# A gated convolution and memory-attention layer: another order for the requests, squares and streamed rows of its output projection, and for its first requests

## What is computed

```
h    = rms_norm(x, pre_norm)
proj = h @ w_in                                 # 1024 -> 3*1024 + 1536 + 512
b, c, u = split(proj[:, :3072]);  z = c * u
mix  = b * (w0*z[t-2] + w1*z[t-1] + w2*z[t])    # short causal convolution
mem_o = softmax(mq @ k.T / sqrt(128)) @ v       # 4 heads over 256 memory rows
y    = (concat(mix, mem_o) * silu(gate)) @ w_out    # 1536 -> 1024
out  = x + rms_norm(y, post_norm)
```

## Time and profile before

| | |
|---|---|
| timed, median of 3 | 2169.3 us (2167.65 to 2175.27) |
| profiled execution | 2171.62 us, span 2169.8 us |
| TensorE matmuls | busy 2150.4 us, 99% of the span, 9792 |
| TensorE weight loads | busy 1781.7 us, 82%, beside the matmuls |
| VectorE | busy 1216.5 us, 56% |
| ScalarE | busy 753.5 us, 35% |
| GpSimd | busy 222.3 us, 10% |
| moved by DMA | 550.35 MB, mean 254 GB/s |

### The profile page before, as it was taken

How to read it: one execution, slowest core, us unless ns; L and a number is a source line. 1 busy time by engine, 2 the same in 40 slices (tenths; PEclk the granted TensorE clock), 3 DMA queues, 4 the chain that set the end, 5 groups by cost and what they waited for, 6 DMA issues and landing times. The chain is left out here.

```text
span 2169.8 us, 26681 instructions
## 1 busy us (share of the span) xinstructions
PE 2150.4 (99%) x9792; PEld 1781.7 (82%) x9792; DVE 1216.5 (56%) x1840; ACT 753.5 (35%) x1330; POOL 222.3 (10%) x377
## 2 busy tenths in 40 slices
PE   9999999999999999999999999999999999999998
PEld 7888888888888888888888888888888788888787
DVE  7858777533335353354345337575754756555565
ACT  6544333411221342221123234535442533333333
POOL 0100000000000111111111000101010111111110
PEclk9999999999999999999999999999999999999999
DMA  7798777677776778998877666666568866665665
GB/s 272 273 328 299 284 269 275 239 247 243 267 231 219 278 255 292 324 328 284 289 239 258 242 222 202 217 196 222 192 207 317 321 223 237 251 244 210 232 230 191
DMA packets 165057, 550.35 MB, mean 254 GB/s; under 512 B 20224, under 2 KB 20256, under 8 KB 164032
## 3 DMA queue, kind: packets, MB, share of 16 engines
q1 hardware_dynamic: 128528, 416.34, 55.3%
q0 software_dynamic: 36400, 132.31, 17.3%
HBM read 404.90 MB, written 143.67 MB: 253 GB/s over the span
## 5 line engine op out<-in xcount | busy, mean ns | idle before, releaser
L1900 PE MATMUL banks<-hop_hi,slots 128*128 128x512 f32 x2184 | 852.0, 390 | 0.5 <-DMA slots<-w_split 0.4
L1901 PE MATMUL banks<-hop_lo,slots 128*128 128x512 f32 x2184 | 850.2, 389 | 0.0
L1902 PE MATMUL banks<-hop_hi,slots 128*128 128x512 f32 x2184 | 849.9, 389 | 0.0
L1900 PEld LDWEIGHTS banks<-hop_hi,slots 128*128 128x128 f32 x2184 | 410.2, 188 | 86.1 <-issue 0.9
L1902 PEld LDWEIGHTS banks<-hop_hi,slots 128*128 128x128 f32 x2184 | 410.0, 188 | 85.5
L1901 PEld LDWEIGHTS banks<-hop_lo,slots 128*128 128x128 f32 x2184 | 410.2, 188 | 82.9
L1900 PE MATMUL banks<-hop_hi,out_slot 128*128 128x512 f32 x448 | 176.1, 393 | 5.1 <-ACT mix L1075 2.0
L1902 PE MATMUL banks<-hop_hi,out_slot 128*128 128x512 f32 x448 | 175.9, 393 | 0.0
L1901 PE MATMUL banks<-hop_lo,out_slot 128*128 128x512 f32 x448 | 175.7, 392 | 0.0
L1489 DVE TENSOR_TENSOR out_slot<-out_raws,out_slot 128x768 fp32r<-128x768 f32 x112 | 107.2, 957 | 100.4 <-ACT out_slot L1000 100.4
L1546 DVE TENSOR_TENSOR u<-banks,u 128x512 f32<-128x512 f32 x54 | 37.3, 690 | 205.8 <-PE banks L1902 205.7
(11 more groups left out here) (206 smaller groups left out, 2720.0 us busy)
## 6 DMA issues: line engine op xcount, KB each, us to landing
slots<-w_split SPq DMA_DIRECT2D x406, 512.0 KB, 4.3
w_split<-slots SPq DMA_DIRECT2D x140, 512.0 KB, 3.5
mw_stream<-mw_kept SPq DMA_DIRECT2D x96, 512.0 KB, 4.6
out_raws<-g_kept POOLq DMA_DIRECT2D x60, 384.0 KB, 6.1
raws<-in_w_in SPq DMA_DIRECT2D x82, 256.0 KB, 5.0
g_kept<-mix POOLq DMA_DIRECT2D x64, 256.0 KB, 5.1
x_res<-in_x POOLq DMA_DIRECT2D x32, 512.0 KB, 5.6
out_x<-x_res POOLq DMA_DIRECT2D x31, 512.0 KB, 3.5
```

The lines of the kernel that those rows point to most:

```text
L1900: nc.tensor.matmul(dst, a, c, start=first, stop=False, skip_group_check=True)
L1901: nc.tensor.matmul(dst, a, d, start=False, stop=False, skip_group_check=True)
L1902: return nc.tensor.matmul(dst, b, c, start=False, stop=last, skip_group_check=True)
```

## The change

The order of requests, of squares and of streamed rows is changed; no arithmetic is.

- TensorE's small matmuls go from 26 to 14, and wait only for `ones`, which VectorE sets in its first instruction. The gains and the weight blocks X11 of pairs 0 and 1 are requested by ScalarE ahead of its other work; the taps by GpSimd after its constants, and they are waited for only where the first convolution needs them. The first piece of x is split ahead of the first weight block.
- The four squares of token tile 0 all come after both halves of the R6 operand; on VectorE the weight sums of R3 and R7 go behind the low halves of R6, and the last weight block's low part between two pairs of norms.
- `mw_stream` has three places, used round by round for single tiles; in each streamed unit one tile is used first and the other ahead of the last tile. SyncE requests tile 0 of (pair 0, R3) and the operand of R4 right after the last unit of the input projection.
- ScalarE and VectorE split the R4 operand in step 4, ahead of the weight block built in that step.
- On GpSimd the four blocks of pair j+1 come ahead of both residual requests, with the store of tile 2j-1 after the first.
- The post norm's gains lie at the place of `junk` and are requested near the end of the last macro; `junk` is in PSUM.

```diff
-WARM = 26
+WARM = 14
-STREAMED = {R5: 0, R3: 2, R2: 3}
-STREAM = [(j, r) for j in range(OUT_PAIRS) for r in STREAMED]
+STREAMED = (R5, R3, R2)
+STREAM = [(j, r, k) for j in range(OUT_PAIRS) for r in STREAMED for k in range(HB)]
...
-        mw_stream = at("mw_stream", Z_AT, [HB, 2, HALF], f32r)
+        mw_stream = [at(f"mw_stream{n}", offset, [2, HALF], f32r) for n, offset in enumerate((Z_AT, Z_AT + 4 * KB, 118 * KB))]
-        junk = at("junk", S_AT, [2, HALF])
+        junk = psum[:, 4:6, :]
...
+            def load_stream(j, r, k):
+                n = STREAM.index((j, r, k))
+                place = n % len(mw_stream)
+                if n >= len(mw_stream):
+                    sp.wait_ge(mw_used, n - len(mw_stream) + 1)
+                sp.dma_start(mw_stream[place][:].bitcast(f32), mw_kept[r, k]).then_inc(mw_stream_dma[place], 16)
...
-            load_first_x(0, 0)
-            load_raw(0, X11)
-            for n in (1, 2, 3):
+            for n in range(HK):
                 load_first_x(0, n)
-            load_raw(1, X11)
...
             for r in (R6, R3, R7, R2):
                 load_out(r)
+            sp.wait_ge(unit_done, FIRST_OUT)
+            load_stream(0, R3, 0)
+            load_out(R4)
+            load_stream(0, R3, 1)
             sp.wait_ge(hop_lo_done, hop_count(OUT, R1))
             load_rows(R7)
-            load_stream(0, R3)
-            load_out(R4)
+            load_stream(0, R2, 0)
             sp.wait_ge(hop_lo_done, hop_count(OUT, R5))
             load_rows(R4)
-            for j in range(OUT_PAIRS):
-                if j:
-                    load_stream(j, R3)
-                load_stream(j, R2)
-                if j + 1 < OUT_PAIRS:
-                    load_stream(j + 1, R5)
+            load_stream(0, R2, 1)
+            for j, r, k in STREAM[HB * len(STREAMED):]:
+                load_stream(j, r, k)
...
             for j in range(OUT_PAIRS):
-                if j:
+                for part in OUT_BLOCKS:
                     if j + 1 < OUT_PAIRS:
-                        load_block(pool, ALL_PAIRS + j + 1, X21)
-                    store_tile(2 * j - 1)
-                    load_residual(2 * j + 1)
-                if j + 1 < OUT_PAIRS:
-                    for block in (X11, X12, X22) if j else OUT_BLOCKS:
-                        load_block(pool, ALL_PAIRS + j + 1, block)
-                if j == 0:
-                    load_residual(0)
-                    load_residual(1)
+                        load_block(pool, ALL_PAIRS + j + 1, part)
+                    if part == X21 and j:
+                        store_tile(2 * j - 1)
+                load_residual(2 * j)
+                load_residual(2 * j + 1)
                 store_tile(2 * j)
-                if j + 1 < OUT_PAIRS:
-                    load_residual(2 * j + 2)
...
-            act.wait_ge(consts_set, 5)
+            act.dma_start(gains[:], in_gains).then_inc(gains_dma, 16)
+            act.dma_start(raw(0, X11), w_in[row_of(0), X11]).then_inc(raw_dma[PLACE[0, X11]], 16)
+            act.dma_start(raw(1, X11), w_in[row_of(1), X11]).then_inc(raw_dma[PLACE[1, X11]], 16)
+            act.wait_ge(consts_set, 4)
             nc.scalar.activation(ysd[:, 0:1], eps[:], ACT.Sqrt)
...
-            square(0, 0)
             half_hi(R6, 0, Y12, 0)
-            square(0, 1)
             half_hi(R6, 1, Y12, 0)
-            square(0, 2)
-            square(0, 3)
+            for c in range(SUB):
+                square(0, c)
             root(0)
...
+                if n == R7:
+                    operand_hi(OUT, R4)
                 ahead(OUT, n)
...
-                if n in (0, 3):
-                    operand_hi(OUT, {0: R2, 3: R4}[n])
+                if n == 0:
+                    operand_hi(OUT, R2)
...
-            first_unit_rest(1, X22)
             norm(1, 0)
             norm(1, 1)
-            weight_sum(DIRECT, R3)
-            weight_sum(DIRECT, R7)
+            first_unit_rest(1, X22)
             norm(1, 2)
             norm(1, 3)
             half_lo(R6, 0, Y12, KT)
             half_lo(R6, 1, Y12, KT)
+            weight_sum(DIRECT, R3)
+            weight_sum(DIRECT, R7)
...
+                if n == R7:
+                    operand_lo(OUT, R4)
                 ahead(OUT, n)
...
-                if n in (0, 1, 4):
-                    operand_lo(OUT, {0: R7, 1: R2, 4: R4}[n])
+                if n in (0, 1):
+                    operand_lo(OUT, {0: R7, 1: R2}[n])
...
-                    at = STREAMED.get(r, HK)
-                    tiles[at:at] = range(HK, HK + HB)
+                    tiles = [HK] + tiles[:-1] + [HK + 1] + tiles[-1:] if r in STREAMED else tiles + [HK, HK + 1]
```

More of the change, by code:

```diff
@@ L400, in trunk @@
         mw_rows_dma = [sem(f"mw_rows_dma{n}") for n in range(PRODUCTS)]
-        mw_stream_dma = [sem(f"mw_stream_dma{n}") for n in range(HB)]
+        mw_stream_dma = [sem(f"mw_stream_dma{n}") for n in range(len(mw_stream))]
         mw_used = sem("mw_used")
@@ L612, in load_rows @@
                 sp.dma_start(mw_kept_rows[r][:].bitcast(f32), mw_kept[r].rearrange("k p h n -> p k h n")).then_inc(mw_rows_dma[r], 16)
-            def load_stream(j, r):
-                n = STREAM.index((j, r))
-                for k in range(HB):
-                    if n:
-                        sp.wait_ge(mw_used, HB * (n - 1) + k + 1)
-                    sp.dma_start(mw_stream[:, k, :, :].bitcast(f32), mw_kept[r, k]).then_inc(mw_stream_dma[k], 16)
+            def load_stream(j, r, k):
[4 more added lines that the diff above has]
+                sp.dma_start(mw_stream[place][:].bitcast(f32), mw_kept[r, k]).then_inc(mw_stream_dma[place], 16)
             def load_unit(p, r):
@@ L788, in _ @@
         def _(pool):
-            pool.dma_start(gains[:], in_gains).then_inc(small_dma, 16)
-            pool.dma_start(conv_w[:], conv).then_inc(small_dma, 16)
-            pool.memset(ones[:], 1.0).then_inc(consts_set, 1)
             pool.memset(eps[:], EPS).then_inc(consts_set, 1)
@@ L930, in _ @@
                         keep_gated(n)
+                        if n == HEADS - 1:
+                            pool.wait_ge(q_lo_done, HEADS)
+                            pool.dma_start(post_gain[:], post_g).then_inc(post_dma, 16)
             keep_block(ALL_PAIRS - 1, R4)
@@ L1215, in first_silu @@
                 nc.scalar.activation(dst, src, ACT.Silu).then_inc(silu_done, 1)
-            act.wait_ge(consts_set, 5)
+            act.dma_start(gains[:], in_gains).then_inc(gains_dma, 16)
+            act.dma_start(raw(0, X11), w_in[row_of(0), X11]).then_inc(raw_dma[PLACE[0, X11]], 16)
+            act.dma_start(raw(1, X11), w_in[row_of(1), X11]).then_inc(raw_dma[PLACE[1, X11]], 16)
+            act.wait_ge(consts_set, 4)
             nc.scalar.activation(ysd[:, 0:1], eps[:], ACT.Sqrt)
+            act.wait_ge(gains_dma, 16)
+            raw_hi(0)
             first_unit_halves(0, X11)
-            act.wait_ge(small_dma, 32)
-            for k in range(HK):
+            for k in range(1, HK):
                 raw_hi(k)
@@ L1671, in memory @@
                         kv_lo(KV_AT.index(step + 1), half)
-            dve.wait_ge(small_dma, 32)
-            dve.wait_ge(consts_set, 5)
+            nc.vector.memset(ones[:], 1.0).then_inc(ones_set, 1)
+            dve.wait_ge(consts_set, 4)
             def first_unit_rest(p, x):
@@ L1723, in first_scale @@
                 nc.vector.tensor_tensor(dst, src, rs_wide[:], ALU.mult).then_inc(first_scaled, 1)
+            dve.wait_ge(gains_dma, 16)
+            raw_lo(0)
             first_unit_rest(0, X11)
-            for k in range(HK):
+            for k in range(1, HK):
                 raw_lo(k)
@@ L1936, in memory_rows @@
                 if r in STREAMED:
-                    pe.wait_ge(mw_stream_dma[k], 16 * (STREAM.index((p - ALL_PAIRS, r)) + 1))
-                    rows = mw_stream
-                else:
-                    if p == ALL_PAIRS and k == 0:
-                        pe.wait_ge(mw_rows_dma[r], 16)
-                    rows = mw_kept_rows[r]
-                return rows[:, k, 0, :], rows[:, k, 1, :]
+                    n = STREAM.index((p - ALL_PAIRS, r, k))
+                    pe.wait_ge(mw_stream_dma[n % len(mw_stream)], 16 * (n // len(mw_stream) + 1))
+                    rows = mw_stream[n % len(mw_stream)]
+                    return rows[:, 0, :], rows[:, 1, :]
+                if p == ALL_PAIRS and k == 0:
+                    pe.wait_ge(mw_rows_dma[r], 16)
+                return mw_kept_rows[r][:, k, 0, :], mw_kept_rows[r][:, k, 1, :]
             def multiply(p, r):
```

19 lines of the change are left out of this document (12 added, 7 removed).

## The result

The changed kernel takes 2159.27 us (median of 5, 2158.12 to 2161.19), the kernel before beside it 2170.80 us (median of 5, 2167.65 to 2179.17). That is 11.5 us less between the medians; the ratio is 0.9945, 95% interval 0.9925 to 0.9966. Eight of the eleven other kernels ran on two other chips; the kernel before had medians of 2170.75, 2171.93 and 2172.64 us on the three, so 1 to 2 us between runs on different chips show little by themselves. 2160.0 had been predicted. The profiled execution of the changed kernel took 2161.19 us, the slowest of its five, with a span of 2159.4.

What follows compares the result with a forecast made beforehand. Matmuls fill 99% of the span, so only TensorE's waits and clock can give time back. From the profiled 2171.6 us, minus 2.2, 3.4, 5.5 and 0.3, it got 2160.2 and predicted 2160.0 us, range 2156.5 to 2164.5.

Steps and rivals of the forecast that it cites:

- The start: Fewer small matmuls, earlier first product and reordered lists up to about 68 us: gain 2.2 us, bounds 1.0 and 3.8.
- the first row squares of tile 1 landing at 22 as before: Sign at the start: rows of token tile 1 still land at 22 us, as another issuing queue adds no bandwidth.
- the wait of 1.8 us ahead of the first spread: At the start: TensorE, due at 22.8, waits 1.8 us and does the spread of token tile 1 at 24.6.
- the wait of 0.9 us: At the start: TensorE waits 0.9 us ahead of the second spread, at 35.95 instead of 38.14, a gain of 2.2.
- The move to the output projection: Pair 0: R4's operand hidden, second R2 tile's wait 1.7 us instead of 2.6; gain 3.4 us, bounds 2.0 and 5.2.
- rival (a): No wait left at the move, start gives 3 us, as queues share landings favouring small ones: 2157.5 us, chance 0.22.
- The stretch around 2030: Output projection: GpSimd's store wait, late blocks, TensorE's waits and half clock go; gain 5.5 us, between 3 and 5.8.
- small waits: Steady pairs of the output projection: deeper streaming takes away small waits of 0.3 us in all.
- the timed runs need not all have it: The loss near 2030 hangs on a slow transfer, so timed runs may lack it; the fastest is 4 us below the profiled.
- (b): Start gives nothing: with 14 small matmuls the clock is still 1.2 GHz when real ones start; 2162.5 us, chance 0.10.
- (c): Output projection: residual requests behind four blocks bunch up, every pair stalls from 14 us to landing; 2190 us, chance 0.03.
- (d): Earlier timed runs lacked the stall near 2030 and new slow transfers strike other waits: 2163 us, chance 0.10.

Runs made afterwards that it cites:

- the repeated kernel: The changed kernel run once more with no edit, beside the kernel before: 2158.69 us (2157.33 to 2159.21), ratio to before 0.9938.

## Why the prediction was right, and where it wasn't

The time came 1.2 us below the forecast, inside the range, with every sign right. That it came so near is partly luck: the terms were too small by 2.7 us in all (11.4 against 2.8 + 5.1 + 6.2 between the two profiles), and the input projection, which the sum left alone, differs by up to 4.4 us among the profiles. The steps, one by one.

**The start: 2.2 predicted, 2.8 between the first two profiles, 2.5 by undoing it, 2.2 between the means of all.** The small matmuls ran from 1.06 to 6.89, ScalarE's requests took 0.41 to 0.46 us and the first real matmul came at 7.13 (forecast 1.0, 6.9, 0.4, 7.0). The part that failed is "the first row squares of tile 1 landing at 22 as before", and with it the wait of 1.8 us ahead of the first spread. The last rows landed at 20.70 us and the spread ran at 23.70 without a wait. That is no accident of one execution: in the nine profiles with the new queues they landed between 20.51 and 20.96, in the four with the old start between 21.23 and 22.94, and at 21.77 when only small matmuls and weight blocks were put back. The second spread came at 35.17, where 35.95 was forecast, with the wait of 0.9 us that was forecast. The matmul at the fifth weight block stands at 65.35 to 65.78 in eight of those nine (the ninth has the old lists) and at 67.29 to 68.41 in the four, so the kernel before had been profiled in an execution with a late start, and 2.2 is what the change gives in the mean. The sum came to it although one term, the rows, was wrong: the spread ran 0.9 us earlier than the 24.6 that it had, which it had named as a bound only.

Was the rule wrong that another issuing queue only saves issue time (the Trainium skill, DMA: Bandwidth & Descriptors, "Issuing engines are not separate DMA queues")? In bytes it was right. The piece of x requested right behind these rows and one weight block landed at 22.96 us in the changed kernel, 23.02 with the old queue, 22.85 before and 22.93 with the whole old start (there with that weight block 0.7 us behind it), so by 23 us nearly the same had been moved in all four. What differed is the order: in the last three part of its packets went ahead of the rows', so that one of the row requests landed 1.9 to 2.8 us behind the one ahead of it, where 1.3 us is the rule. The sum had taken landing in the order of the requests for granted; why the order differs wasn't tested.

**The move to the output projection: 3.4 predicted, 5.1 measured.** The mechanism stands (R4's operand is hidden, and R2's second tile decides), the size was off at the tile. The step that failed is "only the gains (0.5 MB, 1.3 us at that rate) have left the stretch. So it lands at about 1716.8 - 1.3 = 1715.5". Against the start of the output projection that would be 25.2 us; it was 21.9. By the experiments the late gains alone put the tile back by 3.2 us, and the old streaming alone by 1.7 (23.6 us). The sum had priced the gains as bytes ahead of the tile at the full rate; they were another queue's, which took half of the rate and kept the tile's queue behind for longer than its bytes last. The stretch also moved 414 GB/s, where the sum had used 384. So there was no wait of 1.7 us: the outcome of rival (a) for the move is what happened. Queues do share the rate, as it said; that small transfers are favoured, no run shows. The prediction also gave both parts as one sum, without saying that one is worth little unless the other is done; the two kernels with one of them showed it.

**The stretch around 2030: 5.5 and 0.3 for small waits predicted, 6.2 measured.** Right, and by the chain that was named: GpSimd's wait for stores fell from 115.9 us in 30 waits to 2.2 in one. The doubt that "the timed runs need not all have it" stays half answered. All three profiles with the old order have such waits, of 1.0 and 2.0 us at 1934 and 1940, of 1.2 and 2.0 at 2023 and 2030, and of 1.3 and 2.0 at 2110 and 2141: the place differs, the loss was in each. But the fastest of the 26 runs of the kernel before, 2165.21 us, is as fast as the fastest of the 11 with the new order alone beside it, 2165.35, while the slowest are 2178.83 and 2170.13. So some executions seem to escape the loss, and the slow ones are what the old order adds. What it was worth in timed medians ran from 3.0 us alone to 8.7 beside the new streaming; in the profiles, outside pair 0, it was 6.2 to 7.5.

**The other rivals.** (b), no gain at the start, fell: the fifth weight block's matmul came at 65.57 instead of 68.41. What spoke for it was that the moment at which the clock rises differs between runs of one kernel (the Trainium skill, TensorE: Matmul & The Clock Gate, Part 1). The trace agrees: it rose at 6.21 and 6.87 us in the two profiles of the changed kernel. But in all nine profiles with 14 small matmuls it had risen by 6.9 us, and the real ones start at 7.0 to 7.4. (c), residual rows that bunch up: the residual rows take 5.8 us at the median, against 5.5 before and the 14 from which on they would hurt, and no wait of VectorE or TensorE for them appeared. (d) fell by the times. A slip in the chances: all of (a) and a fifth of the forecast's 0.55 are 0.33, not 0.37. Against profiles the forecast was 11.4 us off before; the measured differences are 10.4 and, in the repeated kernel, 14.3. The forecast falls between them because the first contains a loss of chance that the sum didn't have, while the terms of the move and of the stretch around 2030 were too small.

## What to carry to other kernels

Put a request that must wait for a store behind the requests that others wait for, and judge it by the scatter of the timed runs as well as by one profile: the stall wanders from pair to pair. Where two losses end at nearly the same moment, taking one away shows little; price them together, and look at what each edit leaves late. Bytes that nobody needs soon should leave a stretch in which the DMA engines are full before any deeper buffering is tried, also when they are in another queue: moving 0.5 MB of gains was worth 1.6 us here, and a third buffer behind it 0.1.

## What the runs showed of the hardware

- Packets requested behind a transfer in the same queue can go ahead of part of it. With the old start a piece of x requested behind a weight block landed at 22.93 us, the block at 23.62. The last rows landed 1.1 to 2.2 us later than in the changed kernel in the three profiles compared, partly for this, while the bytes moved by 23 us were nearly the same (7.86 to 7.95 MB).
- Two queues with requests pending at a full rate shared it about evenly (0.86 and 0.82 MB in 4 us). So 0.5 MB in one queue, requested 5 us ahead of a tile in the other, delayed that tile by 3.2 us, more than twice the 1.3 us of its bytes.
- TensorE's granted clock fell to 0.50 behind idle times of 2.0 us (near 2030 before, near 2143 with the old GpSimd order) and of 2.2 us (pair 0 with GpSimd's new order and R4's early split), and within such of 2.2 us (GpSimd's new order alone) and 3.8 us (R4 split late). It did not fall behind those of 2.25 and 1.84 us in pair 0 before, nor behind one of 2.0 us at 1940 with the old order and the old streaming, nor behind one of 0.9 us at 35.17 of the changed kernel. Idle time of about 2 us went either way.
- Matmuls that read their weights from slot 0 start about 6 ns further apart than the others, in every kernel here; the 684 of them (38 units of 18) make some 4 us. It isn't the 32 bytes by which the slot's start misses a multiple of 64.
